# A one-core encoder layer: the last output products of cross attention, their router work and the placing of the second routing group in another order

## The reference

```python
    h = h + memory_cross_attention(rmsnorm(h, g_xattn), rmsnorm(mem, g_mem), w_xq, w_xkv, w_xo)
    h = h + hierarchical_moe(rmsnorm(h, g_moe), w_router_group, w_router_expert, w_exp_gate, w_exp_up, w_exp_down)
...
def memory_cross_attention(hn, memn, w_q, w_kv, w_o):
    ...
    o = jnp.einsum('bhtm,bmhd->bthd', p, v).reshape(bsz, t, D_XA)
    return o @ w_o
...
def hierarchical_moe(hn, w_rg, w_re, w_gate, w_up, w_down):
    g_top, g_idx = lax.top_k(softmax(xf @ w_rg), 1)                    # one of 4 groups
    e_top, e_idx = lax.top_k(softmax((xf @ w_re)[g_idx]), 2)           # two of its 8 experts
    out = sum over the two experts of gate * (silu(xf @ w_gate[e]) * (xf @ w_up[e])) @ w_down[e]
```

## Time and profile before

| | us |
|---|---|
| runs (median; all three) | 1297.19; 1294.0, 1297.19, 1301.17 |
| profiled execution, its time | 1299.5 |
| span of its trace | 1298.0 |
| PE busy (share of the span) | 1161.5 (89%) |
| DVE busy | 670.8 (52%) |
| ACT busy | 468.3 (36%) |
| granted TensorE clock, mean | 0.959 of full speed |

### The profile page before, as it was taken

How to read it: one execution, slowest core, us unless ns; L and a number is a source line. 1 busy time by engine, 2 the same in 40 slices (tenths; PEclk the granted TensorE clock), 3 DMA queues, 4 the chain that set the end, 5 groups by cost and what they waited for, 6 DMA issues and landing times.

```text
span 1298.0 us, 18178 instructions
## 1 busy us (share of the span) xinstructions
PE 1161.5 (89%) x6249; PEld 961.9 (74%) x6249; DVE 670.8 (52%) x1291; ACT 468.3 (36%) x970; POOL 252.1 (19%) x375
## 2 busy tenths in 40 slices
PE   4999999999999999999999999999966999999900
PEld 3888888878877888887889787777865887776600
DVE  5323332311116888424365663754657987773267
ACT  5232222200115666111233333543324666663222
POOL 1222222200002222001100000000022333333234
PEclk9999999999999999999999999999977999999955
DMA  8455343763148212452231002000546999999186
GB/s 285 124 186 164 116 159 114 243 155 71 30 94 208 76 25 78 134 178 81 65 86 66 1 1 72 11 33 33 228 175 212 367 370 351 376 363 341 37 332 252
DMA packets 108741, 204.18 MB, mean 157 GB/s; under 512 B 39550, under 2 KB 51838, under 8 KB 108670
## 3 DMA queue, kind: packets, MB, share of 16 engines
q1 hardware_dynamic: 84974, 146.62, 34.7%
q0 software_dynamic: 17280, 44.07, 9.9%
q10 hardware_dynamic: 6416, 12.59, 2.9%
HBM read 163.06 MB, written 55.10 MB: 168 GB/s over the span
## 4 chain that ended last, share of the span: by engine, by line
PE 74%; DMA 9%; DVE 5%; SPq 4%; issue 3%; ACT 3%; POOL 2%; POOLq 0%; DVEq 0%; ACTq 0%
PE bank L503 16%; PE bank L505 16%; PE bank L504 16%; DMA at<-in_w_exp_down 5%; PE bank L1884 4%; PE bank L2085 3%; PE bank L2013 3%; PE bank L1864 3%; PE bank L2071 2%; PE bank L1873 2%; PE bank L1810 2%; PE bank L2022 2%; PE bank L2051 2%; PE bank L1947 1%; DVE at L1736 1%
## 5 line engine op out<-in xcount | busy, mean ns | idle before, releaser
L503 PE MATMUL bank<-at,at 128*128 128x512 f32 (+1 forms) x1208 | 449.1, 372 | 6.1 <-DVE at L498 4.3
L505 PE MATMUL bank<-at,at 128*128 128x512 f32 (+1 forms) x1208 | 438.2, 363 | 0.0
L504 PE MATMUL bank<-at,at 128*128 128x512 f32 (+1 forms) x1208 | 437.5, 362 | 0.0
L503 PEld LDWEIGHTS bank<-at,at 128*128 128x128 f32 x1208 | 229.3, 190 | 42.4 <-DVE at L498 4.8
L505 PEld LDWEIGHTS bank<-at,at 128*128 128x128 f32 x1208 | 228.8, 189 | 35.9
L504 PEld LDWEIGHTS bank<-at,at 128*128 128x128 f32 x1208 | 229.2, 190 | 32.9
L498 DVE TENSOR_TENSOR at<-at,at 128x1024 fp32r<-128x1024 f32 (+3 forms) x160 | 183.7, 1159 | 115.4 <-ACT at L493 110.6
L493 ACT ACTIVATE at<-at 128x1024 fp32r<-128x1024 f32 (+3 forms) x160 | 153.9, 992 | 171.2 <-DVE at L1383 48.6
L796 POOL TENSOR_TENSOR at<-at 128x1 f32<-128x1 f32 x88 | 26.6, 302 | 532.7 <-ACT at L1125 289.1
L2085 PE MATMUL bank<-at,at 128*128 128x512 f32 x156 | 74.2, 597 | 3.3 <-ACT at L1199 3.3
L908 POOL DMA_INDIRECT y_tok<-at,at x39 | 39.9, 1024 | 154.5 <-DVE at L1698 134.9
(11 more groups left out here) (191 smaller groups left out, 1354.5 us busy)
## 6 DMA issues: line engine op xcount, KB each, us to landing
at<-in_w_exp_gate SPq DMA_DIRECT2D x39, 512.0 KB
at<-in_w_exp_up SPq DMA_DIRECT2D x39, 512.0 KB
at<-in_w_exp_down SPq DMA_DIRECT2D x39, 512.0 KB
at<-y_tok SPq DMA_DIRECT2D x24, 512.0 KB, 9.6
xT_hi_all<-at POOLq DMA_DIRECT2D x12, 512.0 KB, 3.9
xT_lo_all<-at POOLq DMA_DIRECT2D x12, 512.0 KB, 5.7
at<-xT_hi_all SPq DMA_DIRECT2D x3, 2048.0 KB, 11.3
at<-xT_lo_all SPq DMA_DIRECT2D x3, 2048.0 KB, 13.1
```

Source lines behind the costliest of these rows:

```text
L503: nc.tensor.matmul(out, w_hi, x_hi, start=(k == 0), stop=False)
L504: nc.tensor.matmul(out, w_lo, x_hi, start=False, stop=False)
L505: last = nc.tensor.matmul(out, w_hi, x_lo, start=False, stop=(k == len(terms) - 1))
```

## The change

Chunk 2's tail is written in another order: `slots 0`, `T 8` and `T 9` stand later, the two products of tile 11 sooner, and `count 1` stands behind all output products and transposes, ahead of the last two router products. The normed rows of the router go round four buffers instead of two, and their squares and normed rows are placed up to three tiles ahead, also in chunks 1 and 2 while softmax is at work. `place_tokens` and `keep_experts` handle both choices in one instruction of twice the width where they had two, `keep_experts(1)` moves behind `choose (2, 3)`, and `one` has two copies, by the parity of the group. To free semaphores, `mem_here` becomes one semaphore and `pad_here` is merged into `bias_here`.

```diff
-        hs = [at(kb, D) for kb in (104, 76)]
+        hs = [at(kb, D) for kb in (104, 76, 124, 72)]
...
-        one = [at(155.25 + 0.5 * k, TG, NE) for k in range(2)]
+        one = [at(kb, 2, TG, NE) for kb in (155.25, 164.25)]
         sel = at(156.25, TG, NE)
-        one_rank = [at(156.75 + 0.5 * k, TG, NE) for k in range(2)]
+        one_rank = at(156.75, 2, TG, NE)
         in_place = [at(158 + 2 * k, TG, P, dt=F32R) for k in range(2)]
-        in_block = [at(162 + 0.5 * k, TG, NE, dt=F32R) for k in range(2)]
+        in_block = at(162, 2, TG, NE, dt=F32R)
...
         count_stage(0)
-        out_group(10, 0), route_group(7), route_T(8), out_group(10, 1), slots_stage(0), route_group(8)
-        out_group(11, 0), route_T(9), count_stage(1), out_group(11, 1), route_group(9), slots_stage(1)
-        route_T(10), route_T(11), route_group(10), route_group(11)
+        out_group(10, 0), route_group(7), out_group(10, 1), route_T(8)
+        out_group(11, 0), slots_stage(0), out_group(11, 1)
+        route_T(9), route_group(8), route_T(10), route_group(9), route_T(11)
+        count_stage(1)
+        route_group(10), route_group(11)
+        slots_stage(1)
         count_stage(2)
         slots_stage(2)
         place = {st: n for n, st in enumerate(stages)}
 
         sq_at, pre_at = {4: 0, 5: 0}, {4: 0}
-        for n in range(6, len(norms)):
+        for n in range(6, 4 + NT):
             sq_at[n] = place["T", n - 2] + 1
+        for n in range(4 + NT, len(norms)):
+            sq_at[n] = place["T", max(n - 4, 3 + NT)] + 1
         for n in range(5, len(norms)):
-            pre_at[n] = place["T", n - 1]
+            pre_at[n] = place["T", n - 1 if n < 4 + NT else max(n - 3, 3 + NT)]
         for n, (kind, t) in enumerate(norms):
             if kind == "moe":
                 after = place["mm", groups.index(("xo", t, 1))] + 1
                 sq_at[n] = max(sq_at[n], after)
                 pre_at[n] = max(pre_at[n], min(after + 1, place["T", n]))
+            if kind != "mem":
+                sq_at[n], pre_at[n] = max(sq_at[n], sq_at.get(n - 1, 0)), max(pre_at[n], pre_at.get(n - 1, 0))
...
-                        ("mm", "route", 7): (1, 0), ("mm", "xo", 10, 1): (1, 1), ("mm", "route", 8): (1, 2), ("mm", "xo", 11, 0): (1, 3)}
+                        ("mm", "route", 7): (1, 0), ("mm", "xo", 10, 1): (1, 1), ("mm", "xo", 11, 1): (1, 2), ("mm", "route", 8): (1, 3)}
...
+        def norm_rows(n):
+
+            kind, t = norms[n]
+            return hs[t % 4] if kind == "moe" else hs[n % 2]
+
         def norm_col(n):
-            return 8 + n if norms[n][0] == "mem" else 4 + n % 2
+            kind, t = norms[n]
+            return 8 + n if kind == "mem" else 12 + t % 4 if kind == "moe" else 4 + n % 2
...
             pool.wait_ge(mm_done, len(groups))
+            pool.wait_ge(xn_stored[2], 16 * NT // 4)
...
                 if what == "sq":
                     wait_source(act, n)
-                    act.wait_ge(nt_done, n - 1)
-                    stored = (n - n_norms["moe", 0]) // 2
-                    if stored > 0:
-                        act.wait_ge(xn_stored[n % 2], 16 * stored)
-                    nc.scalar.activation(hs[n % 2], H[:, norms[n][1]], ACT.Square, scale=D ** -0.5,
+                    kind, t = norms[n]
+                    if kind == "h":
+                        act.wait_ge(nt_done, n - 1)
+                    elif t < 4:
+                        act.wait_ge(nt_done, n_norms["moe", 0])
+                        act.wait_ge(mm_done, n_groups["q", NCH - 1, XH - 1] + 1)
+                    else:
+                        act.wait_ge(nt_done, n - 3)
+                        act.wait_ge(xn_stored[t % 4], 16 * (t // 4))
...
                 rank = bank[6][:, 0:TG * NE].rearrange("p (t e) -> p t e", t=TG)
+                step(nc.vector.tensor_tensor(one_rank, one[g % 2], rank.unsqueeze(1).to_broadcast([P, 2, TG, NE]), ALU.mult))
+                step(nc.vector.tensor_reduce(rank_of[:, :, tiles], one_rank, AX, ALU.add))
+                dve.wait_ge(slots_done, g)
                 for k in range(2):
-                    step(nc.vector.tensor_tensor(one_rank[k], one[k], rank, ALU.mult))
-                    step(nc.vector.tensor_reduce(rank_of[:, k, tiles], one_rank[k], AX, ALU.add))
-                    dve.wait_ge(slots_done, g)
                     nc.vector.tensor_tensor(in_place[k], over_tokens(rank_of[:, k, tiles], P), iota_p.unsqueeze(1).to_broadcast([P, TG, P]),
                                             ALU.is_equal).then_inc(slot_ready, 1)
-                    nc.vector.tensor_tensor(in_block[k], one[k], over_tokens(token[k][:, tiles], NE), ALU.mult).then_inc(slot_ready, 1)
+                    if k == 0:
+                        nc.vector.tensor_tensor(in_block, one[g % 2], token[:, :, tiles].unsqueeze(3).to_broadcast([P, 2, TG, NE]),
+                                                ALU.mult).then_inc(slot_ready, 1)
 
             def keep_experts(g):
 
-                for k in range(2):
-                    step(nc.vector.tensor_tensor(one_rank[k], one[k], iota_e.unsqueeze(1).to_broadcast([P, TG, NE]), ALU.mult))
-                    step(nc.vector.tensor_reduce(first_of[:, k, TG * g:TG * (g + 1)], one_rank[k], AX, ALU.add))
+                experts = iota_e.unsqueeze(1).unsqueeze(1).to_broadcast([P, 2, TG, NE])
+                step(nc.vector.tensor_tensor(one_rank, one[g % 2], experts, ALU.mult))
+                step(nc.vector.tensor_reduce(first_of[:, :, TG * g:TG * (g + 1)], one_rank, AX, ALU.add))
...
+                    if n == 2:
+                        keep_experts(1)
                     place_tokens(n)
-                    if n < 2:
-                        keep_experts(n)
+                    if n == 0:
+                        keep_experts(0)
```

63 lines of the change are left out of this document (32 added, 31 removed).

## The result

The changed kernel took **1285.63 us**, the median of four runs (1285.13 to 1285.98), beside 1295.6 for the kernel before on the same chip (1293.62 to 1301.17, four runs): a ratio of 0.9914, interval 0.9894 to 0.9934. A second comparison, made later among the experiments, gave 1288.88 beside 1296.6 and 0.9947, interval 0.993 to 0.9963. So the kernel is faster, by 10.0 us in the one and 7.7 us in the other; forecast were 9.2 us and 1288.0.

What follows compares the result with a forecast made beforehand. The bound was taken as one serial path in chunk 2's tail: PE, then DVE late for tile 11, then routes at half clock. 8.8 + 0.4 = 9.2 us off 1297.2 gave 1288.0 us, range 1285 to 1294.5.

Steps and rivals of the forecast that it cites:

- term of 8.8: Chunk 2's tail: in the new order the last copy of logits starts at 957.0 instead of 965.84, 8.8 us sooner.
- if the clock is still full: Last two routes: they end at 956.97 provided PE's clock stays full, taking 3.42 us instead of 6.69.
- term of 0.4 for the placing of group 2: DVE behind `count 2`: placing takes 2.6 us instead of 2.98, making the last mask 0.4 us sooner.
- wait ahead of `xo 10, 1`: Chunk 2's tail: PE waits 0.7 us for an addition behind the normed row and placing of group 0.
- Rival 1: Last routes: the clock falls 6.0 us after the last product though PE is busy, losing 3.7 us; 1291.7 us, chance 0.22.
- early rows and four buffers: Router's normed rows: lifting the wait for a store is worth nothing by itself, but lets the rows stand early.
- Chunk 1: Softmax of chunk 1: an early normed row makes DVE late for an addition, shifting all later times by 0.4 us.
- Wide instructions: Placing and keeping on DVE: an instruction of 256 elements takes 0.42 us; four steps and three masks take 3.45.
- the bounds: Width of 256 on DVE: an instruction costs between 0.28 and 0.69 us, part of a gain between 6.2 and 10.7.
- Rivals 2 and 3: Experts' DMA rate hides the gain, 1297.6 us, chance 0.10; clock falls before `xo 10, 1`, 1308 us, chance 0.05.
- The sum: Whole kernel: 8.8 + 0.4 = 9.2 us sooner, the 0.4 loss included, kept until the end; 1288.0 us.

Runs made afterwards that it cites:

- e7: The changed kernel with the squares and normed rows of tiles 0 to 7 back near their old places; 1286.57 us, ratio 0.9929.
- e8: The changed kernel with unread products filling PE's waits behind the last routes, seven of them ahead of `count 2`; 1285.12 us, ratio 0.9923.
- e5: The changed kernel again, no edit; 1288.88 us, ratio 0.9947 to the kernel before.
- e10: The changed kernel with `T 8` ahead of `xo 10, 1`, chunk 1's normed rows late, and unread products in the waits behind the routes; 1286.09 us.
- e4: The kernel before with three unread products in PE's wait ahead of `T 11`; 1292.75 us, ratio 0.9975.
- e12: The changed kernel with `T 8` first, late chunk 1 rows and fewer unread products, three instead of seven ahead of `count 2`; 1283.97 us, ratio 0.9908.
- e11: The changed kernel with the old order of stages put back; 1291.68 us, ratio 0.9964.
- e3: The kernel before with `count 1` alone moved behind `T 11`, and `slots 1` behind the last routes; 1290.67 us, ratio 0.996.

## What of the prediction held, and the step that failed

The kernel is faster for the two reasons that the prediction names: DVE is no longer late for tile 11, and `T 11` and most of the last routes run at the full clock. What failed is a condition of the term of 8.8, "if the clock is still full" to the end of the routes, and with it the size of that term. The term of 0.4 for the placing of group 2 was too large as well.

**The term of 8.8 (order of the tail): right in kind, 1.1 too large.** From the start of `xo 10, 0` to the last copy of logits I had 25.54 against 34.78, which is 9.2 less, or 8.8 with the 0.4 lost ahead of it. It measured 26.65 (926.76 to 953.41), 8.1 less. Up to the last routes it was 22.34 against 22.09. The wait ahead of `xo 10, 1` is 0.72 (forecast 0.7), `T 11` has none. The step that failed is the sentence "the two routes end at 956.97 if the clock is still full": routes and copy took 4.31 instead of 3.45, 0.86 of the 1.1. The clock fell at 952.0, before they ended, and that is 0.61 of it, since they take 3.70 where it stays full (e7). The other 0.25 is there at any clock: in e7 the two routes take 3.50 (950.35 to 953.85, where PE's next row starts), not 3.42, and the copy starts 0.20 behind them, where I had put it at 0.03.

**Rival 1 was half right.** It said that being busy with transposes and router products would not hold the clock, and the clock did fall with PE at 9.67 of 9.67. But it had the clock fall 6.0 us after the last product, at 3.7 us of loss. With the wait of 2.51 gone it fell 9.5 to 13.2 us after, in eleven kernels of the table (in e8 not at all). In the changed kernel and in e5 that is inside the routes, at a price of 0.6 and 0.7; in the others it is at their end or behind them, and costs 0.2 at most (e10). What decides the point within this span no run settles.

The Trainium skill, "TensorE: Matmul & The Clock Gate", Part 1 on the HAM clock gate, has the throttle as the default state, released by sustained matmul activity. The filled waits agree: in e10 unread products brought the clock back, from 0.50 in 954 to 960 to 0.95 in 960 to 964. The changed kernel's 9.67 busy microseconds ahead of the fall do not, and the measurement decides.

**What carried the gain, and in the traces it isn't a sum.** By the stretches, `count 1` behind `T 11` is alone worth 7.3 us, the whole new order 6.7, the rest without the order 4.7 (6.2 without the low stretch in `xo 11, 0`); together 8.3. All three take DVE's placing and keeping away from in front of the addition of tile 11, by order or by making it shorter. Each cuts the wait of 2.51 ahead of `T 11` to 1.64 or less, and each then has `T 11` and both routes at full clock. The clock's share can be had without any of them: 4.0 in e4, forecast as 4.4. This half can be gained only once. The times are too coarse to bear this out: order alone and rest alone come to 4.5 and 4.0 us by their medians, and their sum, 8.5, lies between the two values of the whole change, 7.7 and 10.0. By the times alone the parts could add up. The prediction had both parts of the 8.8 right, but gave them to the order alone, and priced the early rows and four buffers only as what lets it run. By themselves they do much of the same.

**Placing of group 2: 0.4 forecast, 0.19 measured.** DVE is 0.44 sooner as worked out (2.98 became 2.54, 961.46 to 964.00). But the slots products of the first choice used to run beside the masks of the second; now they start at 963.45, when the last mask has begun, and PE goes on to its next work 1.18 after the end of that mask (965.18 after 964.00), where it was 0.93 (977.80 after 976.87). I followed DVE and left PE's side out: 0.25 lost.

**Chunk 1: 0.4 forecast, 0.4 measured** (3.0 against 2.6), and e7 and e10 take it back. **Wide instructions: 0.42 forecast, 0.41 and 0.42 measured**; the four steps with three masks took 3.35, forecast 3.45. Of the bounds, 0.28 and 0.69, neither was near.

**Rivals 2 and 3 did not come.** The experts' stage, from the slot table to the end, is 319.0 against 320.0, and between 316.4 and 320.0 in all fourteen traces, so the gain was kept. The clock stayed at 1.00 across the wait of 0.72.

**The sum.** By the traces the change is worth 8.3 less 0.4 ahead of it, 7.9 us, where I had 9.2. The two comparisons of times, 10.0 and 7.7, stand on either side. The time itself was 2.4 us under 1288.0, although the terms were too large: 1.6 of it because the kernel before took 1295.6 beside the changed one and not 1297.2, and the rest is of the size of the scatter of few runs, as e5's 1288.88 shows. That the time came out so near was luck in part.

## What to carry to other kernels

- Ask of the last small stage ahead of a serial stretch which engine is late for it and why. One stage moved (`count 1`), so that DVE met the last addition with nothing ahead of it, brought 7.3 of the 8.3 us of the stretch in its trace, and 5.2 us by the medians.
- Gains that end the same stall need not add up: a wait and the low clock behind it can be removed only once. Price each part alone, then together. And set a trace beside the times, since the one execution that it shows can be the best of its kernel.
- Unread products in a wait cost nothing only if they fit it at half clock too, since the clock may have fallen ahead of them. Seven took 8.5 us in e10 and put `count 2` 3.2 us later; three in e12 did not.

## What the runs showed of the hardware that was not expected

The granted clock fell while PE was busy without a break. In the changed kernel that was behind 9.67 us of transposes, counts and router products. There are also single low stretches of 3.4 us in the middle of steady work; here is one of the kernel before (columns as in the earlier trace rows):

```profile
724.90:728.30 3.40, 3.40 (x10) 2.66 (x9) 2.60 (x5) 3.23 (x6) 0.93 (x3) 0.50 0.01 2
```

One comes in all fourteen traces (near 390), others come in some (near 28, near 288, one that begins between 721 and 725, and one within `xo 11, 0` in e4 and e11). Ahead of `xo 10, 0` they add up to 3.4 us in the trace after and 10.2 in the trace before, which at half speed explains up to 3.4 of the 4.3 us between them. e4, which has 3.4 as well, starts `xo 10, 0` at 926.75, like the changed kernel. But e3 has 10.2 and starts it at 927.53, so the clock isn't all of that scatter. What sets these stretches off stays open.
